# A hybrid mixer and expert block: the second half's mixer in another order, squares on ACT, picks over 80 sums

## What is computed

```
def ssd_branch(z, xbc, dt_raw, ...):
    ...
    y = (y * jax.nn.silu(z.astype(f32))).reshape(b, s, G, SSD_WIDTH // G)
    y = y * lax.rsqrt(jnp.mean(y * y, axis=-1, keepdims=True) + EPS)
    ...
def diff_attention(q, k, v, ...):
    ...
    q = partial_rotary(rmsnorm(q, qn_w), cos, sin).astype(f32)
    kf = partial_rotary(rmsnorm(k, kn_w), cos, sin).astype(f32)
    ...
    o = rmsnorm(o, subln_w) * (1.0 - lambda_init)
    ...
def peer_ffn(x, w_q, sub_keys, u, v):
    ...
        s_half, i_half = lax.top_k(sc, K)          # 8 heads, 2 halves, K = 16 of 128 keys
        cand = (s_half[:, :, 0, :, None] + s_half[:, :, 1, None, :]).reshape(tb, PEER_HEADS, K * K)
        ...
        top_s, top_pos = lax.top_k(cand, K)
        idx = jnp.take_along_axis(cand_idx, top_pos, axis=-1)
        g = jax.nn.softmax(top_s, axis=-1)
        u_sel = u[idx]
        v_sel = v[idx]
        h = jax.nn.gelu(jnp.einsum('td,thkd->thk', xb, u_sel).astype(f32), approximate=False)
        return jnp.einsum('thk,thkd->td', (g * h).astype(xb.dtype), v_sel)
```

## Time and profile before

| | us |
|---|---|
| median of 3 runs | 1604.84 |
| lowest and highest | 1601.29, 1609.63 |
| profiled execution, its own time | 1606.55 |
| its span in the trace | 1604.7 |
| PE busy in the span | 1424.3 (89%) |
| DVE busy | 1173.5 (73%) |
| ACT busy | 374.5 (23%) |
| POOL busy | 632.8 (39%) |

### The profile page before, as it was taken

The page is one execution under the profiler, slowest core; times in us unless marked ns, Lnnn a source line. Parts: engine busy times, 40 slices in busy tenths (PEclk is TensorE's granted clock), DMA queues, the critical chain, the costliest instruction groups (busy, mean ns, idle before and its releaser), DMA issues.

```text
span 1604.7 us, 16187 instructions
## 1 busy us (share of the span) xinstructions
PE 1424.3 (89%) x5458; PEld 971.8 (61%) x5458; DVE 1173.5 (73%) x2510; ACT 374.5 (23%) x1011; POOL 632.8 (39%) x516
## 2 busy tenths in 40 slices
PE   5998898964788899999789998999999999999991
PEld 5755647542555788888679887887444444444440
DVE  2446344588677789999989898999676675676568
ACT  3222222311220211111166665655000000000000
POOL 0000000214345442223266665666545544445484
PEclk7999899986898999999989999999999999999996
DMA  5333143644679797887789999999999999999998
GB/s 196 105 105 118 54 156 105 221 164 166 210 275 341 275 339 260 267 273 266 232 300 390 391 377 345 385 351 375 383 348 379 375 390 409 379 380 393 409 410 334
DMA packets 140081, 466.62 MB, mean 291 GB/s; under 512 B 14560, under 2 KB 14944, under 8 KB 139232
## 3 DMA queue, kind: packets, MB, share of 16 engines
q0 software_dynamic: 73728, 268.47, 45.0%
q1 hardware_dynamic: 66272, 197.13, 33.3%
HBM read 461.35 MB, written 4.19 MB: 290 GB/s over the span
## 4 chain that ended last, share of the span: by engine, by line
DVE 35%; PE 30%; DMA 23%; issue 6%; POOL 5%; ACT 1%; SPq 0%; DVEq 0%; ACTq 0%; POOLq 0%
DMA UV<-v,IDX 11%; DMA UV<-u,IDX 10%; PE BANKS L519 9%; PE BANKS L692 7%; PE BANKS L513 7%; DVE X L1227 6%; DVE UV L1223 6%; POOL UV L1272 4%; PE BANKS L711 2%; DVE BIG L1069 2%; DVE BIG L1061 2%; DVE BIG L1063 1%; DVE BIG L1106 1%; DVE BIG L1103 1%; DVE BIG L1108 1%
## 5 line engine op out<-in xcount | busy, mean ns | idle before, releaser
L1272 POOL DMA_INDIRECT UV<-u,IDX x248 | 294.0, 1186 | 680.2 <-DVE UV L1223 325.0
L1272 POOL DMA_INDIRECT UV<-v,IDX x239 | 304.8, 1275 | 265.1 <-DVE X L1227 168.2
L1227 DVE SCALAR_TENSOR_TENSOR X<-UV,HG,X 128x1024 f32<-128x1024 f32 x239 | 306.7, 1283 | 102.3 <-DMA UV<-v,IDX 92.1
L1223 DVE SCALAR_TENSOR_TENSOR UV<-UV,Y 128x1024 f32<-128x1024 f32 x248 | 298.0, 1223 | 91.2 <-DMA UV<-u,IDX 89.6
L692 PE MATMUL BANKS<-T 128*128 128x256 f32 x1024 | 232.1, 383 | 0.7 <-ACT BIG L836 0.7
L692 PE MATMUL BANKS<-T,Y 128*128 128x256 f32 x1024 | 232.0, 383 | 0.0
L723 PE MATMUL BANKS<-T,BIG 128*128 128x512 f32 x512 | 226.8, 596 | 3.2 <-DVE BIG L1247 3.2
L723 PE MATMUL BANKS<-Y,BIG 128*128 128x512 f32 x512 | 224.9, 592 | 0.0
L692 PEld LDWEIGHTS BANKS<-T 128*128 128x128 f32 x1024 | 194.4, 193 | 26.5 <-ACT BIG L836 0.9
L692 PEld LDWEIGHTS BANKS<-T,Y 128*128 128x128 f32 x1024 | 194.5, 193 | 25.7
L513 PE MATMUL BANKS<-T,BIG 128*128 128x256 f32 x768 | 185.9, 404 | 8.1 <-ACT BIG L833 6.0
(11 more groups left out here) (232 smaller groups left out, 1113.2 us busy)
## 6 DMA issues: line engine op xcount, KB each, us to landing
T<-u_t SPq DMA_DIRECT2D x64, 512.0 KB, 5.4
Y<-u_t SPq DMA_DIRECT2D x64, 512.0 KB, 6.3
T<-v SPq DMA_DIRECT2D x64, 512.0 KB, 6.8
Y<-v SPq DMA_DIRECT2D x64, 512.0 KB, 6.8
BIG<-w_in SPq DMA_DIRECT2D x24, 1024.0 KB, 7.4
BIG<-w_q SPq DMA_DIRECT2D x16, 1024.0 KB, 7.5
...
```

Of the source, the lines that this page charges most:

```text
L1223: stt(row, row, 1.0, Y[:, n // 4, :], ALU.mult, ALU.mult, accum_out=acc).then_inc(used, 1)
L1227: stt(xb, row, HG[:, n % 2, i % UNIT:i % UNIT + 1], xb, ALU.mult, ALU.add).then_inc(used, 1)
L1272: pool.indirect_dma_start(row_place(k), None, u if kind == "ru" else v, bass.IndirectOffsetOnAxis(IDX[:, b, c:c + 1], 0)).then_inc(row_in[ ...
```

## The change

It does seven things.

1. The second half's mixer is listed in another order. The pick of unit 1 (`r` 2, `r` 3, `y` 1) stood between the `v` projections and `S2` of block 3, ahead of the attention; its three pieces now stand inside the attention, after heads 9, 10 and 12. `S3` 2 stands right behind `S2` 2. Of the rows, 14 instead of 16 stand ahead of `A` 8, 53 instead of 62 ahead of `W` 16, 77 instead of 86 ahead of `gl` 0.
2. Within the attention, each `W` stands one head earlier, `K` 4, 5 at its end, and `K` 6, 7 between `U` 2 and `F` 3.
3. `N` is split. ACT squares the products in PSUM with sums (`nq`), DVE forms the inverse means (`N`), then scales (`n2`); the next head's `B` and `A` go between. PE may overwrite the bank only after `n2`.
4. The squares in `S3`, `q1`, `k1` and the copies of `U` go from DVE to ACT.
5. `choose` adds only the 80 sums that can be among the best 16, in four groups (`COVER`). `keys_of_choice` finds the first key by comparing the place with the 16 first places of the rows, and adding up steps; it merges the two multiplications of 256 into one of 512 and has more small instructions.
6. The exponential of a pick (`e`) and the gelu (`hg`) are steps of their own, placed later on ACT.
7. `FIRSTJ` is 64 instead of 60, and `rows(2)` instead of `rows(1)` follows each pick beside the `gl` tiles, so 60 instead of 50 rows stand there: 137 before the first one-hot group, and 287 at the end of the `u` tiles. In the one-hot stage no `gl` tile is without a group, where four were.

The core of the diff:

```diff
-FIRSTJ = 60
+FIRSTJ = 64
...
+COVER = (0, 2, 16), (2, 4, 8), (4, 8, 4), (8, 16, 2)
...
-        s += [("ru", n * UNIT + k) for k in range(UNIT)] + [("H", n)]
+        s += [("ru", n * UNIT + k) for k in range(UNIT)] + [("e", n), ("H", n)]
+        if n >= LATE - 1:
+            s.append(("hg", n))
...
+    for n in range(LATE - 1):
+        s.insert(s.index(("H", n)) + 24, ("hg", n))
...
+    def attention(first, end, after, between=()):
+        out = on("A", first) + on("A", first + 1) + list(between)
         for i in range(first, end):
+            ended = [i // DH - 1] if i > first and i % DH == 0 else []
+            for b in ended:
+                out += on("nq", b)
             out += on("B", i)
+            for b in ended:
+                out += on("N", b)
             if i + 2 < end:
                 out += on("A", i + 2)
+            for b in ended:
+                out += on("n2", b)
...
-    o += pick(0) + on("z", 2) + on("z", 3) + on("k2", 1) + many("qt", 4, 6) + on("S1", 2) + rows(4) + on("q", 2)
-    o += on("q", 3) + on("S2", 2) + rows(2) + on("S3", 2) + on("q1", 1) + on("S1", 3) + rows(2) + on("q2", 1)
-    o += on("v", 2) + on("v", 3) + pick(1) + on("S2", 3) + rows(4) + on("S3", 3) + rows(4) + many("qt", 6, 8)
...
+    o += pick(0) + on("z", 2) + on("z", 3) + on("k2", 1) + many("qt", 4, 6) + rows(4) + on("S1", 2) + rows(3)
+    o += on("q", 2) + on("q", 3) + on("qs", 1) + on("S2", 2) + on("S3", 2) + on("S1", 3) + on("q1", 1) + rows(2)
+    o += on("q2", 1) + on("v", 2) + on("v", 3) + rows(3) + on("S2", 3) + rows(2) + many("qt", 6, 8) + on("S3", 3)
...
-        work += [first] + rows(2) + [second] + rows(2) + [keys] + rows(1)
+        work += [first] + rows(2) + [second] + rows(2) + [keys] + rows(2)
...
+                elif step == "nq":
+                    act.wait_ge(pv_full, DH * (i + 1))
+                    for h in range(DH):
+                        nc.scalar.activation(TMP[:, 1, h * P:(h + 1) * P], PS[2][:, h * P:(h + 1) * P], ACT.Square,
+                                             accum_out=NSQ[:, i, NG + h:NG + h + 1]).then_inc(o_sq, 1)
...
-                link(tt(CAND.rearrange("p (a c) -> p a c", c=TOPK), bc(TOPV[:, 0, :], 2, TOPK),
-                        bc(TOPV[:, 1, :], 1, TOPK), ALU.add))
+                for first, end, n in COVER:
+                    cand = CAND[:, FIRST_OF[first]:FIRST_OF[first] + (end - first) * n]
+                    last = tt(cand.rearrange("p (a c) -> p a c", c=n), bc(TOPV[:, 0, first:end], 2, n),
+                              bc(TOPV[:, 1, 0:n], 1, end - first), ALU.add)
+                link(last)
```

More of the change, by code:

```diff
@@ L51 @@
 V_MIX, V_SSD, V_SUB, V_CW, V_CB = 0, 8, 12, 13, 13 + CB * CONVW
-NCOLP = V_CB + CB
+V_FIRST = V_CB + CB
+NCOLP = V_FIRST + TOPK
+COVER = (0, 2, 16), (2, 4, 8), (4, 8, 4), (8, 16, 2)
+NCAND = sum((end - first) * n for first, end, n in COVER)
+FIRST_OF = [sum((min(a, end) - first) * n for first, end, n in COVER if first < a) for a in range(TOPK)]
 def bc(ap, axis, n):
@@ L84, in rows @@
         out = []
-        while place[0] < len(stream) and (m or stream[place[0]][0] in ("H", "w")):
+        while place[0] < len(stream) and (m or stream[place[0]][0] not in ("ru", "rv")):
             item = stream[place[0]]
@@ L126, in work_order @@
-    after = {i: many("W", i, i + 1) + rows(3) for i in range(8, 16)}
-    after[11] += on("N", 2)
-    after[12] += many("K", 4, 6) + on("T", 2)
-    after[15] += many("K", 6, 8)
-    after[15] += on("N", 3) + rows(3) + on("R0", 2) + rows(3) + on("R1 Q", 2) + on("T", 3) + rows(2) + on("F", 2)
-    after[15] += rows(3) + on("R0", 3) + rows(3) + on("R1 Q", 3) + on("U", 2) + rows(2) + on("F U", 3) + rows(6)
-    o += attention(8, 16, after)
+    o += many("cv", 14, 16) + many("W", 0, 4) + many("K", 0, 2) + on("ks k1", 1) + many("W", 4, 8) + many("K", 2, 4)
@@ new lines, in work_order @@
+    o += pick(0) + on("z", 2) + on("z", 3) + on("k2", 1) + many("qt", 4, 6) + rows(4) + on("S1", 2) + rows(3)
+    o += on("q", 2) + on("q", 3) + on("qs", 1) + on("S2", 2) + on("S3", 2) + on("S1", 3) + on("q1", 1) + rows(2)
+    o += on("q2", 1) + on("v", 2) + on("v", 3) + rows(3) + on("S2", 3) + rows(2) + many("qt", 6, 8) + on("S3", 3)
+    at_start = many("W", 8, 9) + rows(2)
+    first, second, keys = pick(1)
+    between = {9: [first], 10: [second], 12: [keys]}
+    after = {}
+    for i in range(8, 16):
+        after[i] = (many("W", i + 1, i + 2) if i < 15 else many("K", 4, 6)) + (between[i] if i in between else rows(3))
+        if i == 12:
+            after[i] += on("T", 2)
@@ L335, in block_program @@
         CHOSEN = nth(("r",))
-        EXPS = {s: i for i, s in enumerate(s for s in ORDER if s[0] == "y" and (s[1] < NUNIT or s[1] % 4 == 3))}
+        EXPS = nth(("e",))
+        RAW = {n: m for m, n in enumerate(n for step, n in ORDER if step == "y" and ("e", n) in EXPS)}
         def ring_places():
@@ L823, in _ @@
                                          accum_out=SS[:, i:i + 1]).then_inc(sq_done, 1)
+                elif step == "U":
+                    for c in range(2):
+                        act.wait_ge(ut_full, 2 * i + c + 1)
+                        nc.scalar.activation(T8[:, i // 2, 4 * c:4 * c + 4, i % 2 * P:(i % 2 + 1) * P],
+                                             PS[c][:, :].rearrange("p (i n) -> p i n", n=P), ACT.Copy).then_inc(ut_done, 1)
                 elif step == "F":
@@ L1095, in keys_of_choice @@
                 pos = POS[:, :, :].rearrange("p h k -> p (h k)")
[L1096 to L1098 removed]
+                for m, (first, _, c) in enumerate(COVER[1:]):
+                    ts(PAB[:, m, :], pos, FIRST_OF[first], c, ALU.is_lt, ALU.mult)
+                nc.vector.tensor_copy(PABF[:, 0, :], pos)
+                nc.vector.tensor_copy(STEP[:, :, 0:1], TOPI[:, :, 0, 0:1])
```

206 lines of the change are left out of this document (109 added, 97 removed).

## The result

The changed kernel takes 1563.85 us (median of 4 runs, 1556.66 to 1567.91) where the kernel before takes 1606.43 (4 runs). The ratio is 0.9733, with a 95% interval of 0.9685 to 0.9781; two later comparisons gave 0.9739 [0.9708, 0.9770] and 0.9732 [0.9709, 0.9756]. The forecast was 1562. The profiled execution took 1561.11, its span is 1559.3. Three executions far off all others (1899.44 us of the kernel with the order alone, 5330.16 and 5234.70 of the kernel before) are in none of the ratios.

A forecast was written before the change was run, and what follows sets the result against it. DVE's chain bounds the start of the one-hot stage; DMA and PE bound what follows. Terms -3 - 26 - 8.4 + 0.4 - 1.3 + 0.2 - 5 = -43 us, from a median of 1604.84 to 1562; range 1550 to 1583.

The forecast's parts named there:

- (1): First half: squares leaving DVE bring 2.3 us and the split of N 0 0.7; -3 us in all.
- (2): From the first half to A 8: DVE loses the pick, squares, sums and two rows, PE's waits shrink; -26 us.
- (3): Attention, A 8 to the second output tile: DVE paces it, then PE sets the end; 88.1 to 79.7 us, -8.4.
- (4): Second output tile to W 16: U 2's copies leave DVE, K 6, 7 come in between; +0.4 us.
- (5): 504 to 578 us: pick 1.3 us shorter; PE's 6.0 us wait for ACT goes, but PE isn't the later one; -1.3.
- (6): Hidden-tile stage: r 4.75 us, y about 6.05, ten more rows; +0.2 us, PE still waiting about 12 at its end.
- (7): After the one-hot stage starts: four tiles fewer save 16 us, 8 more rows behind the v stage cost 11; -5 us.
- C: Rival: DVE's gaps only move and the hidden stage starts as late; only (5) to (7) stay, 1599 us; chance 0.04.
- D: Rival: PE's clock falls to 1.2 GHz from the attention to the last W; +91 us, 1653; chance 0.03.
- A: Rival: row transfers from the attention on take back half of (2) and (3), 17 us; 1579 us; chance 0.13.
- B: Rival: small costs at their far ends, y +1.2 us and the 8 rows at 2.19; about 1576 us; chance 0.13.
- E: Better case: half of DVE's 20.7 idle us in 504 to 578 and some attention waits go too; 1548 us; chance 0.05.

The follow-up runs named there:

- the kernel with the order alone: The kernel before with only the new order of the second half's mixer: 1599.82 us, ratio 0.9957 [0.9935, 0.9980].
- the run with the pick ahead: The changed kernel with unit 1's pick whole between the v projections and S2 of block 3, nothing behind heads 9, 10, 12: 1571.65 us, ratio 0.9767.
- The last run: The changed kernel with each W of the attention one head later, behind its own head again: 1562.32 us, ratio 0.9711 [0.9689, 0.9734].
- the order-only pair: The kernel before with the new mixer order, without and with the transfer of the scores moved later: 1599.82 and 1605.69 us.

## Why the prediction was right

The total was right, 43 us forecast and 43 measured. Of its seven terms one, the attention, missed by 7.6 us; the other six were each better or worse by 0.3 to 3.2, together 7.3 us better, and so made up for it. That the parts bring about 40 us is the working's merit; that the total agrees within 1 us is luck. The measured side is the mean of the three profiles of the changed kernel, less the one profile of the kernel before; with the chance start it comes to 45.6.

| step | forecast | measured |
|---|---|---|
| start, up to the first projections | 0 | -2.8, chance |
| (1) to A 0: squares | -2.3 | -2.6 |
| (1), (2) to A 8 | -26.7 | -28.4 |
| (3) attention | -8.4 | -0.8 |
| (4), (5) to the hidden-tile stage | -0.9 | -2.8 |
| (6) hidden-tile stage | +0.2 | +0.7 |
| (7) one-hot stage | -16 | -16.7 |
| (7) v stage and rows behind | +11 | +7.8 |

(1) Right in its mechanism and its size: the run with the squares on DVE gives 2.9 back. The rest of **-3**, 0.7 for `N` 0, stands behind A 0: DVE's difference of head 7 starts 42.8 us behind A 0 in the kernel before and 41.8 in the changed one, 1.0 less. Over ACT but in one piece, by the run with the norms whole, it is 45.4, later than before. So of the 3.1 to 3.8 us that the split brings, most only pays for the squares' way over ACT.

(2) Right. The pick taken from where PE waited 20.7 us came off the path whole: the run with the pick ahead puts it at 16.1 to 18.7 us (13.8 at the least), for 15.6 of DVE's work. A 8 stands at 348.5 and not at 354: 3.7 of these 5 us are the chance start, the rest this step.

(3) Wrong, by 7.6 us. The halves themselves were priced right: heads 10 and 11 come after 9.2 and 9.4 us, where a head with three rows took 8.0 and +1.3 each was forecast. But the sum slipped. `N` stood 35.1 us behind A 8; with 2.3 and twice 1.3 the step's own terms put head 12's difference at 40.0 and head 13's at 54.1. The forecast has 52.8, so it counted the second half of the pick at nothing. With that put right the step is -7.1 and the sum -42.

Three more things were off (the numbers are those of the first profile, where they make 6.1 us). First, the next head, with three rows again, took 9.3: PE had waited 3.48 us and ran at a granted clock of 0.66, and DVE waited for its scores (3.16 ahead of the memset at 384.07 in DVE's timeline). With that head 12's difference began 40.7 us behind A 8 and not 40.0. Second, the end of block 2 took 15.3 us and not 14.0 (13.4 and 15.5 in the other two profiles); my sum of DVE's pieces with "a wait for PE of about 1.0" took DVE as the bound, and the run without the keys of the pick took as long, so PE was. Third, and most (4.2 us; 5.0 in the mean of the three), "Then PE sets the end": from head 13's difference on it took 31.1 us and not 26.9. This is the step that failed. It took a whole W of 3.42 and the `K` of 2.05 off PE's path, but PE waited 1.90 and 2.02 us for DVE's differences of heads 13 and 14, so the W that went had stood beside such waits. The last run puts its place at 1.8 to 2.7 us, not 3.4. And the wait on the second half of `w_out`, 2.15 before, of which I took 1.2 off, was 1.63, 4.12 and 1.51 in the three profiles. What the `K` brought, no run shows. PE's timeline of the changed kernel, the differences of heads 13 and 14:

```profile
405.75 0.66 PE L624 MATMUL BANKS<-CONST,BIG 128*128 128x128 f32 x4 [1.90 <-DVE BIG L1226]
...
414.03 0.72 PE L624 MATMUL BANKS<-CONST,BIG 128*128 128x128 f32 x4 [2.02 <-DVE BIG L1226]
```

The split of the norms was right: in one piece they cost some 3.4 us in this stretch.

(4), (5) The sizes are within what these stretches vary by. The step's reason, "PE isn't the later one here", holds: 10 us less of PE's waiting in the order-only pair did not bring DVE forward. DVE waits for row transfers there.

(6) Right to 0.5 us: r 4.80, y 6.00, and 12.4 us back with 256 sums. (The step's terms -19.0, +6.0 and +13.0 add up to 0.0, not +0.2.) The small instructions do start 0.11 apart (551.39 and 551.50 in DVE's timeline); the Trainium skill's fixed cost ("VectorE: DVE Perf Modes", The TRN2 errata), set end to end, would have made the 26 `r` 7 us dearer, and the trace doesn't show it. A side remark was wrong: PE's wait ahead of the one-hot stage is 5.7, 7.8 and 9.2 in the three profiles, not 12. I let PE start earlier against DVE. In the first profile both came forward nearly alike (41.4 and 42.6 us), and four tiles took 14 of its 17.6.

(7) Right in its mechanism, with the second term too large. Of the 8 rows fewer at the v stage 5 to 6 are done behind it (DVE has 31, 30 and 31 instructions in the last window where it had 25), and that stretch is 7.4 us longer and not 11, the v stage 0.4. The 29 us that the forecast starts from are DVE's busy time there; the stretch was 31.5.

Of the rivals, C (the gaps only move) and D (PE's clock stays down) are refuted. But D's mechanism is seen on a small scale, in the 10 us behind the second half of the pick. A, the row transfers, is seen where (5) stands: the stretch varies by 6 us in the changed kernel, but it never took the 17 back. B was not needed: `y` came out at 6.00, and the rows behind cheaper than forecast. E, the better case, did not come: the stretch before the hidden-tile stage gave 2.8 us. The other rule of the Trainium skill, that multiplications should stay on VectorE ("ScalarE: Activation LUTs", Rules for kernel authors), would have had `n2` held up by `nq` for some 4 us (its factor of 3 is for bf16, and these squares are float32). DVE waited 0.63 us for it in block 2 and 3.17 in block 3, where PE had the output projection of block 2 to do. And putting the other squares back on DVE made 2.9 us up to A 0, and 4 to 7 us of the time with overlapping intervals.
